# A third Strassen block in eight gate and up couples, and four exponentials moved by one chunk

## The reference, cut to what matters

```python
hf = rms_norm(x, g_ffn)
gg, uu = jnp.split(hf @ w_gu, 2, axis=-1)
return x + (jax.nn.silu(gg) * uu) @ w_down
...
s = jnp.einsum('bkgtd,bksd->bkgts', qb, kw).astype(f32)
s = jnp.where(okw, s - sl5 * dw.astype(f32), NEG)
p = jax.nn.softmax(s, axis=-1)
o_win = jnp.einsum('bkgts,bksd->bkgtd', p.astype(vw.dtype), vw)
```

## Time and profile before

| | |
|---|---|
| median of 3 runs | 2369.03 us (2365.76, 2369.23, 2369.03) |
| the profiled execution | 2366.16 us |
| its span, first to last instruction | 2364.9 us |
| TensorE busy | 2357.1 us, 11163 matmuls |
| VectorE busy | 1808.4 us (76%) |
| ScalarE busy | 1215.0 us (51%) |
| DMA, mean | 192 GB/s, 453 MB |
| TensorE clock granted | full in all slices |
| gate and up couples 1 to 9 | 43.11 to 43.13 us each |

### The profile page before, as it was taken

How to read it: one execution, slowest core, us unless ns; L and a number is a source line. 1 busy time by engine, 2 the same in 40 slices (tenths; PEclk the granted TensorE clock), 3 DMA queues, 4 the chain that set the end, 5 groups by cost and what they waited for, 6 DMA issues and landing times.

```text
span 2364.9 us, 28701 instructions
## 1 busy us (share of the span) xinstructions
PE 2357.1 (100%) x11163; PEld 1955.2 (83%) x11163; DVE 1808.4 (76%) x2614; ACT 1215.0 (51%) x1537; POOL 0.2 (0%) x4
## 2 busy tenths in 40 slices
PE   9999999999999999999999999999999999999999
PEld 8888888888888888888888887888888888888887
DVE  5565999867777877877757866876888878869776
ACT  5554444544544555554555555546555555545554
POOL 0000000000000000000000000000000000000000
PEclk9999999999999999999999999999999999999999
DMA  8645666666565666676645545564566666665664
GB/s 273 205 143 183 191 194 191 216 190 210 192 203 161 215 212 201 196 269 213 185 145 156 161 139 206 171 182 142 175 201 195 196 196 187 196 205 182 224 201 160
DMA packets 126100, 453.00 MB, mean 192 GB/s; under 512 B 13899, under 2 KB 16636, under 8 KB 124684
## 3 DMA queue, kind: packets, MB, share of 16 engines
q1 hardware_dynamic: 125964, 451.17, 60.2%
HBM read 448.99 MB, written 2.12 MB: 191 GB/s over the span
## 4 chain that ended last, share of the span: by engine, by line
PE 98%; DVE 1%; ACT 1%; DMA 0%; SPq 0%; issue 0%; ACTq 0%
PE ps L1470 16%; PE ps L1472 16%; PE ps L1471 16%; PE ps L1511 14%; PE ps L1513 14%; PE ps L1512 14%; PE ps L972 2%; PE ps L1005 1%; PE ps L986 1%; PE ps L1316 1%; PE ps L996 0%; DMA t_raw<-w_in 0%; PE ps L1115 0%; DVE t_wlo L2965 0%; PE ps L1546 0%; ACT t_whi L2054 0%
## 5 line engine op out<-in xcount | busy, mean ns | idle before, releaser
L2965 DVE TENSOR_TENSOR t_wlo<-t_raw,t_whi 128x1024 fp32r<-128x1024 f32 (+1 forms) x800 | 939.0, 1187 | 425.2 <-ACT t_whi L2054 420.0
L2054 ACT ACTIVATE t_whi<-t_raw 128x1024 fp32r<-128x1024 f32 (+1 forms) x800 | 822.9, 1032 | 824.4 <-PE ps L1472 458.3
L1470 PE MATMUL ps<-t_whi,t_A 128*128 128x512 f32 (+1 forms) x1324 | 525.7, 397 | 0.4 <-DVE t_wlo L2965 0.3
L1472 PE MATMUL ps<-t_wlo,t_A 128*128 128x512 f32 (+1 forms) x1324 | 513.1, 388 | 0.0
L1471 PE MATMUL ps<-t_whi,t_A 128*128 128x512 f32 (+1 forms) x1324 | 512.1, 387 | 0.0
L1511 PE MATMUL ps<-t_whi,t_A 128*128 128x512 f32 x1014 | 396.8, 391 | 0.0
L1513 PE MATMUL ps<-t_wlo,t_A 128*128 128x512 f32 x1014 | 394.8, 389 | 0.0
L1512 PE MATMUL ps<-t_whi,t_A 128*128 128x512 f32 x1014 | 394.5, 389 | 0.0
L1470 PEld LDWEIGHTS ps<-t_whi,t_A 128*128 128x128 f32 x1324 | 248.9, 188 | 52.3 <-issue 4.4
L1472 PEld LDWEIGHTS ps<-t_wlo,t_A 128*128 128x128 f32 x1324 | 248.6, 188 | 51.8
L1471 PEld LDWEIGHTS ps<-t_whi,t_A 128*128 128x128 f32 x1324 | 249.1, 188 | 46.3
(11 more groups left out here) (402 smaller groups left out, 2439.7 us busy)
## 6 DMA issues: line engine op xcount, KB each, us to landing
t_raw<-w_in SPq DMA_DIRECT2D x371, 512.0 KB, 4.1
t_raw<-w_gu SPq DMA_DIRECT2D x176, 512.0 KB, 3.9
t_raw<-w_down SPq DMA_DIRECT2D x88, 512.0 KB, 3.8
t_raw<-w_branch SPq DMA_DIRECT2D x64, 512.0 KB, 4.2
t_raw<-w_out SPq DMA_DIRECT2D x64, 512.0 KB, 4.2
t_raw<-w_ck SPq DMA_DIRECT2D x16, 512.0 KB, 4.3
t_raw<-w_cv SPq DMA_DIRECT2D x16, 512.0 KB, 4.4
t_raw<-w_cq SPq DMA_DIRECT2D x8, 512.0 KB, 3.5
```

Of the source, the lines that this page charges most:

```text
L1470: te.matmul(ps[:, 0:n], u.op.hi[:, x, tok], h[:, k, :], start=(kt == 0), stop=False)
L1472: made = te.matmul(ps[:, 0:n], u.op.hi[:, x, tok], l[:, k, :], start=False, stop=(kt == u.kts - 1))
L2054: se.activation(whi[:, k % NH, 0:n], raw_of(d)[:, 0:n], ACT.Copy).then_inc(*hi.up((d, 1)))
L2965: ve.tensor_tensor(wlo[:, k % NH, 0:n], raw_of(d)[:, 0:n], whi[:, k % NH, 0:n].bitcast(F32), ALU.subtract).then_inc(*lo.up((d, 1)))
```

## The change

FEED is the order of the eleven couples. Couples 1 to 8 get three blocks instead of two and so 5 plain chunks of each unit instead of 6; couples 0, 9 and 10 stay. The new third block lies one chunk earlier in the contraction (rows 1280 to 1535), so `feed_in` makes a second, smaller set of activation sums, R[1], in the first half of tile M0. `emptied` now lets TensorE reuse the banks of a mixed couple when `gather` has read them, and no longer only when the result has been multiplied. In AT one number of nsa_part1 goes from 53001 to 53101; the other changed numbers follow the new count of chunks (22 in a couple, 20 before), or place the second set.

```diff
-FEED = ("aaaaaabbb0b3b1b2ab",) + ("aaaa0b3a1b20b3b1b2ab",) * 9 + ("a" * 8 + "b" * 8,)
+FEED = ("aaaaaabbb0b3b1b2ab",) + ("aa0b3a1b20b3a120b312ab",) * 8 + ("aaaa0b3a1b20b3b1b2ab",) + ("a" * 8 + "b" * 8,)
...
     nsa_part1=[51102, 51114, 51314, 51400, 51401, 51402, 51501, 51502, 51814, 51900, 51902, 51914, 51914, 52014,
-        52301, 52302, 52314, 52414, 53000, 53001, 53400, 53401, 53402, 53414, 53414, 53500, 53814, 53900, 54014,
+        52301, 52302, 52314, 52414, 53000, 53101, 53400, 53401, 53402, 53414, 53414, 53500, 53814, 53900, 54014,
...
-    feed_in=[60000, 60002, 60014, 60100, 60114],
+    feed_in=[60000, 60002, 60014, 60100, 60114, 60202, 60214, 60314, 60400, 60414],
...
-    R32 = [at("M1", [2, 4, P]), at("R0", [2, 4, P], off=4096)]
+    R32 = [[at("M1", [2, 4, P]), at("R0", [2, 4, P], off=4096)], [at("M0", [1, 4, P], off=2048 * i) for i in range(2)]]
...
-        W, e = (S, c) if i in (11, 12) else (XS, c - 5) if i in FRONTS else (R, c - 6)
+        W, e = (S, c) if i in (11, 12) else (XS, c - 5) if i in FRONTS else (R[0], c - 6) if c > 5 else (R[1], c - 5)
...
-        if name in paired and paired[name][0] in FRONTS:
+        if in_sevens(u):
             return made_s["dve"].at(f"C{2 * paired[name][1] + t} {paired[name][0]}")
...
+            for i, k in enumerate((slice(12, 16), slice(10, 12))):
+                whole, s = R32[i]
...
```

More of the change, by code:

```diff
@@ L133 @@
     front_out=[22314, 22314, 24314, 24314, 26314, 26314, 29314, 29314, 32314, 32314, 35314, 35314, 38314, 38314],
-    feed_in=[60000, 60002, 60014, 60100, 60114],
[L135 to L139, removed]
+    feed_in=[60000, 60002, 60014, 60100, 60114, 60202, 60214, 60314, 60400, 60414],
+    feed_out=[61014, 61014, 63214, 63214, 65414, 65414, 67614, 67614, 69814, 69814, 72014, 72014, 74214, 74214, 76414,
+        76414, 78614, 78614, 80614, 80614],
+    down_in=[82514, 82614, 82714, 82800, 82814, 83414, 83614, 83814, 84000, 84114, 84814, 85014, 85214, 85400, 85514],
+    down_out=[87214, 87214, 87314, 87314, 87414, 87414, 87514, 87514, 93214, 93214, 93214, 93314, 93314, 93314, 93414,
+        93414])
 class Marks:
@@ L365, in body @@
     sums = at("H6", [2, 1024])
-    R32 = [at("M1", [2, 4, P]), at("R0", [2, 4, P], off=4096)]
-    R = [at("M1", [2, 4, P], F32R), at("R0", [2, 4, P], F32R, 4096)]
+    R32 = [[at("M1", [2, 4, P]), at("R0", [2, 4, P], off=4096)], [at("M0", [1, 4, P], off=2048 * i) for i in range(2)]]
+    R = [[at("M1", [2, 4, P], F32R), at("R0", [2, 4, P], F32R, 4096)],
+         [at("M0", [1, 4, P], F32R, 2048 * i) for i in range(2)]]
     cross_sums = [at("M0", [NT, 512], off=4096), at("R0", [NT, 512])]
@@ L469, in body @@
     z_s = signals("z", turned(*range(0, 44, 2)), turned(*range(0, 44, 2)), turned(*range(0, 44, 2)))
-    made_s = signals("made", "", ["front hi"] + [f"P1 {i}" for i in FRONTS] + ["feed hi"] + [f"P1 {i}" for i in MIXED] + each(len(MADE), "hi")
+    made_s = signals("made", "", ["front hi"] + [f"P1 {i}" for i in FRONTS] + ["feed hi0", "feed hi1"] + [f"P1 {i}" for i in MIXED] + each(len(MADE), "hi")
                      + ["P1 11", "P1 12"], ["front sums", "front lo"]
-                     + [f"{x} {i}" for i in FRONTS for x in "U V W V5 C0 C1 C2 C3".split()] + ["feed sums", "feed lo"]
+                     + [f"{x} {i}" for i in FRONTS for x in "U V W V5 C0 C1 C2 C3".split()] + ["feed sums0", "feed lo0", "feed sums1", "feed lo1"]
                      + [f"{x} {i}" for i in MIXED for x in "U V W V5 C0 C1 C2 C3".split()] + each(len(MADE), "sums", "lo")
@@ L1498, in down @@
                     pe.wait_ge(*made_s["dve"].at(f"lo{piece}"))
-                elif op is R:
-                    pe.wait_ge(*made_s["dve"].at("feed lo"))
+                elif op in R:
+                    pe.wait_ge(*made_s["dve"].at(f"feed lo{R.index(op)}"))
                 elif op is XS:
@@ L1991, in feed_in @@
         def feed_in():
[L1992 to L1998, removed]
+            for i in range(2):
+                yield
+                yield
+                yield
+                act.wait_ge(*made_s["dve"].at(f"feed sums{i}"))
+                se.activation(R[i][0][:], R32[i][1][:], ACT.Copy).then_inc(*made_s["act"].up(f"feed hi{i}"))
+                yield
+                yield
         def couple_out(these):
@@ L2833, in feed_in @@
         def feed_in():
[L2835 to L2852, removed]
@@ L2853, in feed_in @@
-            yield
+            for i, k in enumerate((slice(12, 16), slice(10, 12))):
+                whole, s = R32[i]
+                a11, a21, a12, a22 = (whole[:, :, j, :] for j in range(4))
+                dve.wait_ge(*fop_s["dve"].at("t14"))
+                ve.tensor_tensor(whole[:].rearrange("p c (k t) n -> p (c k) (t n)", k=2), fop.hi[:, k, :].bitcast(F32),
+                                 fop.lo[:, k, :].bitcast(F32), ALU.add).then_inc(*dve_step.up())
+                yield
+                dve.wait_ge(*dve_step.last())
+                ve.tensor_tensor(s[:, :, 0, :], a21, a22, ALU.add).then_inc(*dve_step.up())
+                ve.tensor_tensor(s[:, :, 2, :], a11, a21, ALU.subtract)
+                yield
+                dve.wait_ge(*dve_step.last())
+                ve.tensor_tensor(s[:, :, 1, :], s[:, :, 0, :], a11, ALU.subtract).then_inc(*dve_step.up())
+                dve.wait_ge(*dve_step.last())
+                ve.tensor_tensor(s[:, :, 3, :], a12, s[:, :, 1, :], ALU.subtract).then_inc(
+                    *made_s["dve"].up(f"feed sums{i}"))
+                yield
+                yield
+                dve.wait_ge(*made_s["act"].at(f"feed hi{i}"))
+                ve.tensor_tensor(R[i][1][:], s[:], R[i][0][:].bitcast(F32), ALU.subtract).then_inc(
+                    *made_s["dve"].up(f"feed lo{i}"))
+                yield
```

## The result

| | before | changed |
|---|---|---|
| median of 6 runs each | 2368.43 us (2365.76 to 2370.92) | 2380.02 us (2378.16 to 2381.28) |
| the profiled execution | 2366.16 us | 2378.16 us |
| its span | 2364.9 us | 2376.9 us |

The ratio is 1.0045, with a 95% interval of 1.0035 to 1.0056: the changed kernel is slower by some 11 us (10.7 by the ratio, 11.6 by the medians). 2374.5 us had been forecast, 5.5 us above the median of before as it stood then (2369.03), with a range up to 2379.5; the sign came out as forecast, the size was about twice the forecast one, and the median lies 0.5 us above the end of the range.

The account below looks back on a forecast made before the run. TensorE's products by their spacing, plus waits, were taken to bound the kernel. Waits of 10.9 us less 5.4 gained, plus 0.6 for exponentials, made 6.0 us on 2366.16 or 2369.03; forecast 2374.5 us, range 2366.5 to 2379.5.

Parts of the forecast that it names:

- Products: Gate and up couples 1 to 8: 24 matmuls fewer on TensorE at 0.2267 us each, 5.44 us gained.
- The boundary: Between couples, VectorE's queued weight sums make TensorE wait for b: 1.33 us at 7 boundaries, 1.09 at the first.
- The third block: Inside a changed couple, the third block's part 0 waits for VectorE's split: 0.06 us each, 0.5 us in all.
- Exponentials: Near 1450 us, moved exponentials remove 1.2 us of waits but delay the second transposes: +0.6 us, bounds -1.2 and +2.
- The clock: TensorE's clock is at full speed in every slice; no time was put down for it.
- No new waits: VectorE keeps ahead in the changed couples, so only fewer products count: 2362.4 to 2364.2 us, chance 0.14.
- Half the wait: At the boundary b is late by 0.6 to 0.9 us, gain just paid back: 2368 to 2372 us, chance 0.24.
- Late loads: Part 0's sums wait for a slow raw tile load, 0.5 us in each of 8 couples: 2378.5 us, chance 0.10.

Follow-up runs that it names:

- the new order: Changed kernel with couples 1 to 8 in the order abab03a1b203a12b0312ab, gated transposes moved, exponentials in their old place: 2363.88 us median, ratio 0.9975 to the kernel before.
- the sums made small: Changed kernel with the four weight sums of the first block in couples 1 to 8 only 16 columns wide instead of 512: 2368.22 us.
- the order alone: Kernel before, two blocks kept, couples 1 to 8 opening with two plain gate chunks instead of four, with the changed bank rule: 2380.95 us.
- the sums put back: Changed kernel, three blocks kept, couples 1 to 8 opening with four plain gate chunks as before: 2368.48 us.

## Why the prediction was right in its sign and short in its size

**Products: right.** -0.68 us per couple; the new order, which has no waits, shows 43.12 to 42.45, so -5.4 us in all.

**The boundary: the mechanism right, the term too small.** The count from t = 1779.23 (TensorE's start of part 3 of the last block) held to the row: first split at t + 1.29 as said, b's low half ready at t + 16.95 where I had 16.97, b started at t + 17.01. Three runs show it: the sums made small (-1.51 us), the order alone (+1.28 us without any added work), the sums put back (-1.5 us). The term was 1.33 us; at TensorE's starts it is 1.37 + 0.10, and by the length of couples 1.51. The 0.10 is the late second product after a wait, which no step of mine had. The last 0.04 I can't place in rows; spacings of a hundredth of a us longer would make it. Over eight boundaries: 11.8 us where I had 10.4.

**The third block: the step that failed.** I had: "1.29, a split, four sums, a split, 6.18 us, against 27 products, 6.12 us: 0.06 us". It costs 0.45 to 0.47 us, 3.8 us in all for 0.5. The rows at 1814.28 show why. The four sums start 1.36 us after the split ahead of them, not 1.14, though VectorE has nothing else to do. That split, of part 2, still reads t_H, the tile that the sums write, and `sums_of` makes the first sum wait until it is done; an operation without such a wait starts while the one ahead of it ends. That is 0.22 us. From the start of part 0's split to TensorE's start are 1.28 us, not 1.22, and 0.11 go at the restart: 6.46 + 0.11 - 6.12 = 0.45. A second t_H wasn't tried; that the wait goes away with another order is shown, that it goes with another buffer isn't.

**Exponentials: right.** +0.6 forecast, +0.58 shown: the eight traces without a dip in that stretch fall in two groups, three with the old place and five with the new. The wait that was to vanish did, and the one forecast ("one of 1.5 to 2 us for ScalarE's exponential at about 1451") came at 1.72 us, its end at 1452.59.

**The clock: a term I had at zero.** I wrote that the clock is at full speed in every slice; a 9 in the page's row says only 90% or more, over 59 us. A dip of 1.65 us is in the changed kernel's trace and none is in that of before, so 1.65 of the 12.0 us come of it. It can't be put to the change: the kernel before with only its order and bank rule changed, and the exponentials in their old place, had three. The trace of before was the exception: all 13 executions of that kernel that were run beside the experiments list a mean clock of 0.999 or 0.998, which the traces here have with one to three dips, and it lists 1.000. The six executions of the changed kernel list 0.999 four times and 0.998 twice. So the 2.9 us by which the median lay above the trace of before, which I added without a cause, may well be dips. Without the clock and the scatter at the start the account is 10.2 + 0.6 = 10.8 us, near the 10.7 to 11.6 measured.

So the changed couples' windows were forecast at 43.7 to 43.8 us and came out at 44.43; 5.44 is subtracted rightly, 15.6 us of waits stand where 10.9 were written. With 0.6 for the exponentials, 1.65 for the clock and -0.5 at the start that makes the 12.0 us.

**The rivals.** No new waits: excluded by TensorE's 16 waits. Half the wait: excluded too, b's queue was as long as counted, to 0.04 us. Late loads: the load that the sums need went out at t + 3.68, where I had t + 3.6, and landed 4.34 us later, 1.65 us before the sums; these start back to back behind the gathers at 1788.90, and making them small removed the boundary's cost with all loads in place.

## What to carry to other kernels

An engine with reserve on average can still hold up the stream: list its queue in order from the last moment at which it was held back, and compare each due time, since 36 us of work in a bad order cost 1.28 us a couple here and 40 us in a good one cost nothing. A new piece of work belongs where the queue has slack before the next due time, and if a gap is tight to 0.1 us, count as well the operation that overwrites what the one ahead of it still reads, and the restart. Look at the granted clock in windows of a few us before a difference of 1 or 2 us is put down to an edit.

## What the runs showed of the hardware

- **Short clock dips on a busy TensorE.** Nine of the ten traces have one to three, each costing 1.65 us: in all nine between 1476 and 1488 us, in two more between 1452 and 1458 and in two between 1192 and 1197 us. In the changed kernel TensorE had no idle time in the windows from 1468 us on; ahead of the fall it was doing 32 narrow products of 15 columns, then scores. Products of 512 columns start 0.43 us apart in a dip. The Trainium skill ("TensorE: Matmul & The Clock Gate", Wait — 56ns, not 53.3ns?) gives the columns over 1.2 GHz for the lower level, 427 ns here: the traces agree. The same page (What's actually happening) calls the half rate the state of an idle TensorE; these rows mark it busy for 4.00 of 4.00 us as the clock falls, so they differ: being marked busy doesn't keep the clock. Executions without a kept trace have the dips too: the mean clock that each lists is 1.000 in the trace without a dip, 0.999 in those with one or two and 0.998 in those with three, and of the 13 executions of the kernel before beside the experiments nine list 0.999 and four 0.998. Their times overlap (2367.2 to 2370.8 and 2368.8 to 2371.0), so the dips are not all of the scatter. What makes the clock fall was not tested.
- **A restart costs twice.** After each pause for a low half the second product comes 0.10 to 0.11 us late, and after a group of transposes 0.08 to 0.09.
- **A wait for the operation just ahead, on VectorE.** A 1024-wide split is followed after 1.14 us by an operation that doesn't wait for it and after 1.36 us by a sum that does, since it overwrites what the split reads; among the 512-wide sums the step is 0.60 us, and 0.72 where the next one waits for what the last one wrote (1790.10 to 1790.82).
